# A two-block transformer kernel in float32: h_lo's last two tiles lie 32 bytes further down

## The chip, the cores and the metric

The kernel runs on one core of a Trainium2 chip. The time is that of the device from start to end, in microseconds (us), as the median of three runs. Besides the times there is one profiled execution, from which all rows below are taken.

## The reference, cut to what matters

Two transformer blocks are computed on 256 tokens of width 2048, all in float32. What the change touches is the left factor of most of the large products, h:

```python
def pool_mixer_layer(x, norm_g, w_in, w_group, scale, w_out):
    h = rmsnorm(x, norm_g)
    proj = h @ w_in                      # 2048 x 8192
    ...
def mla_layer(x, k, v, ...):
    h = rmsnorm(x, norm_g)
    proj = h @ w_in                      # 2048 x 2560
    ...
    return x + (o * jax.nn.silu(gate)) @ w_out
def second_block(x, c, ...):
    h = rms_norm(x, norm_attn[l]) * (1.0 + sc1) + sh1
    qa, ka, va, qb, ckv, qi, ki, wi = jnp.split(h @ w_in[l], SPLIT_POINTS, axis=-1)
    ...
    h = rms_norm(x, norm_ffn[l]) * (1.0 + sc2) + sh2
    x = x + g2 * conv_ffn(h, w_up[l], conv_w[l], conv_b[l], w_down[l])   # 2048 x 11264, 5632 x 2048
    return rms_norm(x, norm_final)
```

## The kernel before, in words

A float32 product is made of three products of a narrower type, float32r. Each factor is split into a high part and a low part; hi x hi, lo x hi and hi x lo are summed. The weights stream in from memory in slabs of 2 x 512 columns (or 4 x 256). SyncE's queue loads a slab into `raw`, ScalarE writes its high part `w_hi` (line 660), VectorE the low part `w_lo` (line 1228), each in a ring of four. The activations are kept transposed, as 16 tiles of 128 features by 256 tokens, in `h_hi` and `h_lo`. They are filled anew for each layer, two tiles at a time, by ScalarE (`h_hi`) and VectorE (`h_lo`, lines 1295, 1298 and 1649), which is the only way in which VectorE is concerned with the change.

`gemm` makes one product of four output tiles. It goes over eight slabs, and slab s uses the tiles 2s and 2s + 1 of h. Within a slab there are 16 matmuls with `w_hi`, which alternate between `h_hi` and `h_lo`, and then 8 with `w_lo`, which read `h_hi` alone. The weights are the stationary factor, and the tile of h (256 columns, 1024 bytes in each partition) is the moving one. All are issued by the helper on line 1953. Slabs of 4 x 256 columns use four tiles of h and give two output tiles, so the third and the fourth tile alternate with the first and second. Products whose moving factor is something else (`pool`, `y`, `y_mid`, `f`, `hk`, `c`, `q`, `mixw`) are made in the same manner; `hk_hi` and `hk_lo` are a copy of h for the key and value product and lie in two other homes.

The order on each engine is written out by hand, with semaphores. It runs through the first layer (from the start to about 630 us in the profile), key and value product and attention layer (to about 1010 us), the second block's attention (to about 1330 us) and its FFN, the feed-forward part (to the end). The small matmuls of the attention stages are put between the slabs.

The memory is laid out by hand as well: `home(start, end)` gives addresses in order, each tensor at a multiple of 32 bytes. From H_AT = 147776 on there are `h_hi` and `h_lo`. Both are `Parted`: the first 14 tiles, a gap of 8 floats (32 bytes), the last two tiles under the name `..._tail`, and a gap behind. So `h_hi` takes 16640 bytes and `h_lo` begins at H_AT + 16640. `Parted` picks the tensor by the index of the tile; no access goes over the boundary. In what follows the slab of tiles 14 and 15 is called the tail slab.

Of the kernel before, what the change touches and what calls it, by code (L numbers as in the profile page):

```python
# [16 lines left out]
F32R = mybir.dt.float32r  # L17
# [5 lines left out]
P = 128  # L23
TOK = 256
HALVES = TOK // P
D = 2048
KD = D // P
# [177 lines left out]
def two_block_kernel(nc, t, out, cols):  # L205

    fixed = ExitStack()
    with fixed:
        def home(start, end):

            at = [start]

            def sb(name, shape, dt=F32):
                tile = nc.alloc_sbuf_tensor_at(name, shape, dt, offset=at[0])
                at[0] += -(-4 * int(np.prod(shape[1:])) // 32) * 32
                assert at[0] <= end, (name, at[0], end)
                return tile

            return sb
# [34 lines left out]
        h_sb = home(H_AT, FAR)  # L254
        def h_parts(name, gap):

            main = h_sb(name, [P, H_TAIL, TOK], F32R)
            h_sb(name + "_gap", [P, 8])
            tail = h_sb(name + "_tail", [P, KD - H_TAIL, TOK], F32R)
            h_sb(name + "_end", [P, gap])  # L260
            return Parted(main, tail, H_TAIL)

        h_hi = h_parts("h_hi", 56)
        h_lo = h_parts("h_lo", 8)
        mod_sb = home(MOD_RAW_AT, SB_END)
        mod_raw = [mod_sb(f"mod_raw{s}", [P, 1024]) for s in range(MOD_RING)]

# [2323 lines left out]
```

How the kernel before makes its waits and increments, by code:

```python
            def load_mod():  # L455
                top = LATE_MODS if slabs.total() < LATE_MODS_AT else 6 * MOD_TILES
                while mod_loads.total() < MOD_RING or mod_loads.total() < min(top, MOD_RING + mod_due(slabs.total() - RING - 1)):
                    n = mod_loads.total()
                    if n == LATE_MODS:
                        sp.wait_ge(att[1]["mix_lo"], TILES)
                        load_row()
                    v, j, slot = n // MOD_TILES, n % MOD_TILES, n % MOD_RING
                    if n >= MOD_RING:
                        sp.wait_ge(mod_used, n + 1 - MOD_RING)
                    sp.dma_start(mod_raw[slot][:, :], t["w_mod_2"][bass.ds(v * D + (j // 2) * P, P), bass.ds((j % 2) * 1024, 1024)])\
                        .then_inc(mod_landed[slot], 16)
                    mod_loads.step()
# [1 line left out]
            def load(src, k, n):  # L470
                sp.wait_ge(lo_ready, slabs.value(1))
                s = slabs.slot(RING)
                sp.dma_start(raw[s][:, 0:k * n].rearrange("p (k n) -> p k n", k=k),
                             src.rearrange("(k p) n -> p k n", p=P)).then_inc(raw_landed[s], 16)
                after_load()
# [1 line left out]
            def load_heads(src):  # L478
                sp.wait_ge(lo_ready, slabs.value(1))
                s = slabs.slot(RING)
                sp.dma_start(raw[s][:, :].rearrange("p (h d) -> p h d", d=HD), src.rearrange("h p d -> p h d")).then_inc(raw_landed[s], 16)
                after_load()
```

## Time and profile before

| | us |
|---|---|
| median of three runs | 2078.72 |
| lowest and highest | 2076.68, 2080.64 |
| profiled execution | 2075.5 |
| its span, first to last instruction | 2073.7 |
| TensorE busy in it | 2049.6 |
| VectorE busy | 1566.9 |
| ScalarE busy | 1030.2 |

The profile is a page with tables, and views of the trace behind it. In the page and the views PE is TensorE's matmuls, PEld its loads of weights, DVE VectorE, ACT ScalarE. A row of a group reads: line, engine, operation, output and inputs, shapes, count, then busy time and the mean duration of one in ns, then the idle time before them and what ended it. Matmuls overlap, so that the duration of one is longer than the distance to the next. In a row of the timeline the first number is the start in us, the second the time to the end, and the last the number of equal instructions merged in it.

### The profile page before, as it was taken

The page shows a single profiled execution, that of the slowest core. Times are in us where ns is not written, and L with a number is a line of the kernel's source. Part 1 is how long each engine was busy: PE and PEld are TensorE (multiplying, and loading weights), DVE is VectorE, ACT ScalarE, POOL GpSimd, SP SyncE. Part 2 cuts the span into 40 slices and gives each one's busy share as a digit, 9 for nine tenths or more (in the row PEclk, how much of TensorE's full clock was granted, in tenths as well). Part 3 has the DMA queues.
Part 4 walks back from the last instruction along what each step waited for, and adds up shares of the span by engine and source line. Part 5 has one row for each costly group of instructions (what it writes and reads, how often), then busy time and mean ns, then how long its engine had stood idle before and what let it go on. Part 6 is the DMA issues. An engine that isn't in the chain of part 4 may idle for free.

```text
span 2073.7 us, 41240 instructions
## 1 busy us (share of the span) xinstructions
PE 2049.6 (99%) x17698; PEld 2019.0 (97%) x17698; DVE 1566.9 (76%) x2256; ACT 1030.2 (50%) x1339; POOL 15.4 (1%) x23
## 2 busy tenths in 40 slices
PE   8999999999999999999999999999999999999998
PEld 7999999999999999999999899999999999999998
DVE  7988788688688888877756686778866666666666
ACT  6444444444445476664567557454444444444444
POOL 1000000000000000000000000000000000000000
PEclk9999999999999999999999999999999999999999
DMA  8898888889686788748654754568866666666663
GB/s 272 293 354 278 292 306 304 260 288 324 225 296 204 236 302 297 232 163 280 202 158 120 191 170 135 191 225 321 317 215 192 195 193 193 193 193 193 194 193 122
DMA packets 248749, 483.01 MB, mean 233 GB/s; under 512 B 26347, under 2 KB 59735, under 8 KB 248311
## 3 DMA queue, kind: packets, MB, share of 16 engines
q1 hardware_dynamic: 247807, 480.16, 71.3%
q8 instruction: 139, 2.28, 0.4%
q14 instruction: 43, 0.35, 0.1%
q0 software_dynamic: 528, 0.15, 0.0%
q10 hardware_dynamic: 232, 0.06, 0.0%
HBM read 478.17 MB, written 8.44 MB: 235 GB/s over the span
## 4 chain that ended last, share of the span: by engine, by line
PE 93%; DVE 4%; ACT 1%; DMA 1%; issue 0%; DVEq 0%; SPq 0%; ACTq 0%
PE acc L1953 87%; PE side L1953 3%; PE sums L1953 2%; DVE w_lo L1228 2%; PE sums L2228 1%; DVE tmp L1283 0%; DVE mod_raw L1216 0%; ACT w_hi L660 0%; DMA raw<-in_a_w_in 0%; DVE h_lo L1295 0%; DVE tmp L1285 0%; DVE xT L1358 0%; PE sums L2036 0%; DVE h_lo L1298 0%; PE acc L2088 0%
## 5 line engine op out<-in xcount | busy, mean ns | idle before, releaser
L1228 DVE TENSOR_TENSOR w_lo<-raw,w_hi 128x1024 fp32r<-128x1024 f32 x681 | 830.6, 1229 | 412.8 <-ACT w_hi L660 406.0
L660 ACT ACTIVATE w_hi<-raw 128x1024 fp32r<-128x1024 f32 x681 | 718.3, 1059 | 817.9 <-PE acc L1953 704.4
L1953 PE MATMUL acc<-h_hi,w_hi 128*128 128x256 f32 x3166 | 749.5, 280 | 6.8 <-ACT h_hi L744 2.4
L1953 PE MATMUL acc<-h_lo,w_hi 128*128 128x256 f32 x3166 | 741.1, 277 | 0.0
L1953 PEld LDWEIGHTS acc<-h_hi,w_hi 128*128 128x128 f32 x3166 | 594.7, 189 | 17.4 <-issue 12.7
L1953 PEld LDWEIGHTS acc<-h_lo,w_hi 128*128 128x128 f32 x3166 | 593.4, 188 | 0.1
L1953 PE MATMUL acc<-h_hi,w_lo 128*128 128x256 f32 x3166 | 430.0, 278 | 0.2 <-DVE w_lo L1228 0.2
L1953 PEld LDWEIGHTS acc<-h_hi,w_lo 128*128 128x128 f32 x3166 | 392.9, 188 | 0.4 <-DVE w_lo L1228 0.4
L1216 DVE SCALAR_TENSOR_TENSOR mod_raw<-mod_raw,silu_row 128x1024 f32<-128x1024 f32 x192 | 234.1, 1219 | 5.4 <-DMA mod_raw<-in_w_mod 5.3
L1953 PE MATMUL acc<-f_hi,w_hi 128*128 128x256 f32 x704 | 164.6, 277 | 0.0
L1953 PE MATMUL acc<-f_lo,w_hi 128*128 128x256 f32 x704 | 164.3, 276 | 0.0
L1953 PEld LDWEIGHTS acc<-f_hi,w_hi 128*128 128x128 f32 x704 | 132.2, 188 | 0.1
L1953 PEld LDWEIGHTS acc<-f_lo,w_hi 128*128 128x128 f32 x704 | 132.2, 188 | 0.0
L1953 PE MATMUL acc<-h_hi_tail,w_hi 128*128 128x256 f32 x434 | 105.6, 281 | 0.0
L1953 PE MATMUL acc<-h_lo_tail,w_hi 128*128 128x256 f32 x434 | 105.5, 281 | 0.0
L1953 PE MATMUL acc<-f_hi,w_lo 128*128 128x256 f32 x704 | 94.2, 276 | 0.0
L1953 PE MATMUL acc<-y_hi,w_hi 128*128 128x256 f32 x384 | 89.5, 276 | 0.0
L1953 PE MATMUL acc<-y_lo,w_hi 128*128 128x256 f32 x384 | 89.5, 276 | 0.0
L1953 PEld LDWEIGHTS acc<-f_hi,w_lo 128*128 128x128 f32 x704 | 86.4, 188 | 0.0
L1953 PEld LDWEIGHTS acc<-h_hi_tail,w_hi 128*128 128x128 f32 x434 | 81.6, 188 | 0.5 <-issue 0.5
L1953 PEld LDWEIGHTS acc<-h_lo_tail,w_hi 128*128 128x128 f32 x434 | 81.5, 188 | 0.0
L1953 PEld LDWEIGHTS acc<-y_hi,w_hi 128*128 128x128 f32 x384 | 72.1, 188 | 0.0
(350 smaller groups left out, 2485.1 us busy)
## 6 DMA issues: line engine op xcount, KB each, us to landing
mod_raw<-in_w_mod SPq DMA_DIRECT2D x192, 512.0 KB, 6.4
raw<-in_w_up SPq DMA_DIRECT2D x176, 512.0 KB, 4.4
raw<-in_a_w_in SPq DMA_DIRECT2D x128, 512.0 KB, 5.1
raw<-in_w_down SPq DMA_DIRECT2D x88, 512.0 KB, 4.5
raw<-in_a_w_out SPq DMA_DIRECT2D x64, 512.0 KB, 5.6
raw<-in_w_in SPq DMA_DIRECT2D x52, 512.0 KB, 3.8
raw<-in_b_w_in SPq DMA_DIRECT2D x40, 512.0 KB, 5.1
raw<-in_a_w_group SPq DMA_DIRECT2D x32, 512.0 KB, 5.2
```

The source lines that it names most:

```text
L660: last = act.activation(w_hi[s][:, :], raw[s][:, :], ACT.Copy)
L1216: dve.scalar_tensor_tensor(x[:, :], x[:, :], 1.0, silu_row[:, half * 1024:(half + 1) * 1024], ALU.mult, ALU.mult, accum_out=mod_part[:, v ...
L1228: last = dve.tensor_tensor(w_lo[s][:, :], raw[s][:, :], f32(w_hi[s][:, :]), ALU.subtract)
L1953: return pe.matmul(o, lhsT, rhs, start=start, stop=stop, skip_group_check=True)
L2228: last = pe.transpose(o[:, e, c], pr[:, e, c], ident)
```

## The change

`h_lo` becomes one tensor of 16 tiles. It begins at the same address as before; its tiles 0 to 13 stay where they were, and its tiles 14 and 15 lie 32 bytes further down, right behind tile 13. `h_hi` keeps its gap. Nothing lies behind `h_lo` that would move: the next home has a fixed address. No instruction is added or removed, and no order is changed.

```diff
         h_hi = h_parts("h_hi", 56)
-        h_lo = h_parts("h_lo", 8)
+        h_lo = h_sb("h_lo", [P, KD, TOK], F32R)
         mod_sb = home(MOD_RAW_AT, SB_END)
```

## Rows read from the trace of the kernel before

**Rows 1.** The page: span, busy time and shares of engines, chain that ended last.

```profile
span 2073.7 us, 41240 instructions
...
PE 2049.6 (99%) x17698; PEld 2019.0 (97%) x17698; DVE 1566.9 (76%) x2256; ACT 1030.2 (50%) x1339; POOL 15.4 (1%) x23
...
PE 93%; DVE 4%; ACT 1%; DMA 1%; issue 0%; DVEq 0%; SPq 0%; ACTq 0%
```

**Rows 2.** Costliest groups of the page: count, busy us, mean ns, idle before.

```profile
L1953 PE MATMUL acc<-h_hi,w_hi 128*128 128x256 f32 x3166 | 749.5, 280 | 6.8 <-ACT h_hi L744 2.4
```

**Rows 3.** Windows: stretch, its us, PE busy (x matmuls), clock, DMA share, GB/s.

```profile
28.00:630.00 602.00, 601.78 (x5274) 1.00 0.85 290
...
655.00:1330.00 675.00, 670.36 (x5667) 1.00 0.67 210
...
1359.00:2054.00 695.00, 695.00 (x6106) 1.00 0.68 212
```

**Rows 4.** Groups of PE within 655 to 1330 us.

```profile
L1953 PE MATMUL acc<-h_hi,w_hi 128*128 128x256 f32 x1024 | 249.8, 286 | 3.3 <-DVE kq L1530 1.5 <-ACT h_hi L744 1.2 <-DVE xT L1358 0.7
```

**Rows 5.** Tile h_lo_tail: count, duration ns min/median/max, first and last start.

```profile
L1953 PE MATMUL acc<-h_lo_tail,w_hi x434: 277/281/285, 35.9 to 2014.3; 128*128 128x256 f32 x144, 128*80 128x256 f32 x1
L1298 DVE SCALAR_TENSOR_TENSOR h_lo_tail<-tmp,mod,h_hi_tail x4: 479/486/488, 1024.1 to 1347.3; 128x256 fp32r<-128x256 f32 x4
```

**Rows 6.** Timeline of PE (start us, us) in the FFN, round a tail slab.

```profile
1486.88 1.07 PE L1953 MATMUL acc<-h_hi,w_lo 128*128 128x256 f32 x8
1487.79 0.28 PE L1953 MATMUL acc<-h_hi_tail,w_hi 128*128 128x256 f32 x1
...
1489.68 1.11 PE L1953 MATMUL acc<-h_hi_tail,w_lo 128*128 128x256 f32 x8
1490.62 0.28 PE L1953 MATMUL acc<-f_hi,w_hi 128*128 128x256 f32 x1
...
1491.22 0.28 PE L1953 MATMUL acc<-f_lo,w_hi 128*128 128x256 f32 x1
...
1498.82 0.28 PE L1953 MATMUL acc<-f_hi,w_hi 128*128 128x256 f32 x1
...
1501.54 0.28 PE L1953 MATMUL acc<-f_hi,w_hi 128*128 128x256 f32 x1
```

**Rows 7.** The same, where the FFN begins.

```profile
1355.55 1.10 PE L1953 MATMUL acc<-h_hi,w_lo 128*128 128x256 f32 x8
1356.49 0.28 PE L1953 MATMUL acc<-h_hi_tail,w_hi 128*128 128x256 f32 x1
...
1359.33 0.29 PE L1953 MATMUL acc<-h_hi,w_hi 128*128 128x256 f32 x1
...
1361.18 1.07 PE L1953 MATMUL acc<-h_hi,w_lo 128*128 128x256 f32 x8
```

**Rows 8.** The same, a slab of four rows of tiles (12 to 15).

```profile
1213.36 0.28 PE L1953 MATMUL acc<-h_hi,w_hi 128*128 128x256 f32 x1
...
1213.81 0.28 PE L1953 MATMUL acc<-h_hi_tail,w_hi 128*128 128x256 f32 x1
...
1214.28 0.28 PE L1953 MATMUL acc<-h_hi,w_hi 128*128 128x256 f32 x1
...
1214.75 0.28 PE L1953 MATMUL acc<-h_hi_tail,w_hi 128*128 128x256 f32 x1
...
1215.22 0.40 PE L1953 MATMUL acc<-h_hi,w_lo 128*128 128x256 f32 x2
```

**Rows 9.** The same, first slab of the key and value product.

```profile
630.57 0.28 PE L1953 MATMUL acc<-hk_hi,w_hi 128*128 128x256 f32 x1
...
632.43 1.07 PE L1953 MATMUL acc<-hk_hi,w_lo 128*128 128x256 f32 x8
```

**Rows 10.** The same, products over y: five slabs in a row.

```profile
185.85 1.07 PE L1953 MATMUL acc<-y_hi,w_lo 128*128 128x256 f32 x8
...
196.73 1.07 PE L1953 MATMUL acc<-y_hi,w_lo 128*128 128x256 f32 x8
```

## The prediction

> **What bounds the kernel now.** I read the page first, for who is busy: of a span of 2073.7 us TensorE works 2049.6 us, and 93% of the chain that ended last is its own [rows 1]. VectorE, the next, has 24% to spare. The largest matmul group has 6.8 us of idle time before it for 749.5 us of work [rows 2]. Then the windows: from 28 to 630 us and from 1359 to 2054 us TensorE is busy all the time at the full granted clock, which is the level of 2.4 GHz, while the DMA share is 0.85 and 0.68 [rows 3]. So in these 1297 us nothing ends last but TensorE's own stream, and the time is the number of matmuls times the distance between two starts. 695.00 us over 6106 matmuls is 113.8 ns each [rows 3]. The durations of some 280 ns are of no use for this, since matmuls overlap; what counts is the distance of starts, the **pace**, and it is read from the timeline.
>
> **The pace** has more than one value. A slab (24 matmuls of 256 columns: 16 with w_hi, 8 with w_lo) of f tiles runs from 1498.82 to 1501.54, 2.72 us, 113.3 ns a matmul. The slab of tiles 14 and 15, the tail slab, runs from 1487.79 to 1490.62, 2.83 us or 117.9 ns, and its 16 matmuls with w_hi, from 1487.79 to 1489.68, take 118.1 ns each [rows 6]. Is it the place of the tiles in memory, or that this is the last slab of a product, when the other engines turn to the sums? The products over y answer: four slabs each, so one in four is a last one, and four slabs in a row take 196.73 - 185.85 = 10.88 us, 2.72 each, the last one included [rows 10]. The place remains. H_AT is 64 x 2309, and h_lo starts at H_AT + 16640 = 64 x 2569; main tiles lie at multiples of 64 bytes, tail tiles 32 bytes past one.
>
> Two more things can be seen. After a tail slab the first five matmuls, which read f tiles at multiples of 64, take 1490.62 to 1491.22, 120 ns each, and then the pace is 113.3 again [rows 6]. And the slow pace also occurs where nothing is shifted: the eight matmuls of tiles 12 and 13 with w_lo before 1356.49 need 0.94 us, 117.5 ns, and eight after the tail slab need 1.07 us from first start to last end instead of 1.10 [rows 7]. So TensorE has a fast and a slow pace for the same tiles, it stays in the one that it is in, and the tail slab, itself slow, was followed by the fast one. The FFN (the feed-forward part) then keeps it for 695 us.
>
> **The change part by part.** It removes the 32-byte gap between h_lo's tiles 13 and 14. h_lo's main tiles, h_hi with its tail and all else stay where they are: h_lo starts at the same address before and after. No instruction, wait, queue or size is added or taken away. What moves is the operand of 434 matmuls with w_hi [rows 5] and the target of seven VectorE instructions that fill the tail tiles, such as the four of 486 ns [rows 5].
> - Those seven: I take their cost as nothing, since their inputs and sizes are the same. If each were 5% longer or shorter, at about half a microsecond each, and all of it on the path, that is 7 x 0.025 = 0.2 us either way.
> - The 434 matmuls. 49 slabs have 8 of them, nine slabs of four tiles each have 4, one narrower slab has 6: 392 + 36 + 6 = 434. In each such stretch a matmul of h_hi's tail, still shifted, alternates with one of h_lo's, no longer shifted; the 8 with w_lo read h_hi's tail alone and are as before. No row shows this very mixture. **Lower bound:** every h_lo matmul falls to the fast pace and its neighbours don't change: 434 x (118.1 - 113.3) ns = 2.1 us less. **Upper bound:** a matmul at a multiple of 64 after a shifted one costs what the five after a tail slab do, 120 ns, and so does its partner: 868 x 1.9 ns = 1.6 us more [rows 6].
> - Between these, two nearer rows. The slab of tiles 12 to 15 changes between places every four matmuls: its first four, unshifted, take 0.45 us (112 ns each), the four shifted 0.47, the next four unshifted ones 0.47 as well, not 0.45, and the next shifted four 0.47 [rows 8]. Once disturbed, unshifted tiles run at 117.5 ns among shifted ones, so a mixture gains next to nothing. The key and value product alternates, matmul by matmul, between two homes, hk_hi at FAR and hk_lo at MID, and its 16 with w_hi take 632.43 - 630.57 = 1.86 us, 116.3 ns each, 1.8 below the tail's [rows 9]; by this row the change saves 868 x 1.8 ns = 1.6 us. The first row is nearer, having the same tiles and the same 32 bytes; the second is nearer in its rhythm. I take 0.5 us less, and keep -2.1 to +1.6.
> - The slab after the tail: the last 8 matmuls before it, all on h_hi's shifted tail, are unchanged, so I leave its 16 with w_hi at 1.85 us [rows 7], 0.04 above the fast pace. If this goes away, 50 times 0.04 is 2 us less; the reverse is the rival below.
>
> The Trainium skill speaks against any effect. SBUF — State Buffer, under Specifications (TRN2), gives SBUF lines of 16 bytes and a penalty for each move to another line. By that rule a tile of 1024 bytes covers 64 lines with the shift and without it, so the change would do nothing. The 118.1 against 113.3 ns of rows 6 don't agree with it.
>
> **Sum.** The profiled execution took 2075.5 us, its span of 2073.7 and 1.8 around it. Minus 0.5 it is 2075.0. The median of the three runs is 2078.72, 3.2 above the profiled one; minus 0.5 it is 2078.2. The runs themselves differ by 4 us (2076.68 to 2080.64), so this gain would not be seen: about 0.2%, 4.2 us, is what a measurement of this kernel can tell from no change.
>
> **The rivals.**
> 1. Place plays no part, and the tail slab is slow for another reason, or the lines of 16 bytes are all that counts. Then the time is as before, 2078.7. Rows 10 speak against it; it moves neither sign.
> 2. The slow side: **the tail slab no longer hands over the fast pace.** The shifted stretch is what precedes the change to the fast pace in rows 7. Now its first 16 matmuls are mixed, and the 8 shifted ones left may be too few to bring it about. The place is the slab after each tail slab; it decides as soon as that slab keeps 117.5 to 118 ns instead of returning within five matmuls. In the FFN 21 tail slabs after 1359 hold 504 of 6106 matmuls; the other 5602 at 4.4 ns more make 24.6 us. From 28 to 630 us 5274 matmuls less 16 tail slabs (384) and the 384 on y_mid leave 4506, or 19.8 us [rows 3]. Both: 2078.7 + 44.4 = 2123; one alone: about 2100. Against it: rows 6 and 7 show the handover from a fast and from a slow state alike, and rows 8 show shifted and unshifted tiles mixed without the slab growing slower than a tail slab. For it: nothing in the trace has this mixture followed by eight shifted ones.
> 3. The fast side: from 655 to 1330 us TensorE often falls into the slow pace after small matmuls of the attention stages. There 1024 matmuls of h_hi with w_hi [rows 4] have as many of h_lo and of w_lo beside them, 3072, up to 4.4 ns too slow each, 13.5 us. A different tail could draw these anew. If half of it goes, with the 2.1 us above, the time is about 2070; the same redraw can lose, since not all of the stretch is slow.
>
> **How the numbers follow.** Forecast (mixture between the bounds, handover kept) 0.72; rival 1 0.08; rival 2 0.12, of which half is the whole 44 us; rival 3 0.07; 0.01 is left for losses of another kind. The likeliest is the forecast: 2078.2 us. Its own range is the bounds, -2.1 to +1.6, with 2 us for the runs on either side: 2074.6 to 2082.3. To hold 8 in 10 a little of the redraw in the middle is taken in: 2074.0 to 2084.0; the whole of rival 2 stays outside. Within 0.2% (2074.6 to 2082.9) lie the forecast and rival 1 nearly whole, 0.79; faster are rival 3 and a sliver, 0.08; slower 0.13.
>
> **What would show it.** In the changed trace a tail slab's 16 matmuls with w_hi take 1.86 to 1.91 us. 1.85 or less says that the two places are paid for separately (lower bound). The slab after it: its eight with w_lo take 1.07 us if the handover holds, 1.10 if rival 2 is right, and the window of the FFN is then about 720 us instead of 695. Rival 3 shows between 655 and 1330 us only. If tail slabs keep 118.1 ns to the tenth while h_lo lies at a multiple of 64, the pace is set by h_hi alone or by something other than place. The prediction is wrong as soon as the FFN's pace leaves 113.8 ns.

## The result and the profile after

| | before | after |
|---|---|---|
| median, four runs each on one chip (us) | 2078.85 | 2096.9 |
| lowest and highest | 2076.68, 2080.64 | 2091.66, 2101.38 |
| profiled execution, its span | 2075.5, 2073.7 | 2101.38, 2099.5 |

The ratio is 1.0092 (95% interval 1.008 to 1.0104): 18 us slower. The forecast was 2078.2 us, within 2074 to 2084. It was wrong. The profiled execution of the changed kernel is the slowest of its four, while that of the kernel before is faster than any of its four, so the two traces differ by 25.8 us where the medians differ by 18. What follows explains the 25.8; why executions of one kernel differ by up to 10 us was not traced.

The page of the changed kernel: the span, the busy times, the chain that ended last, and three groups (busy us, mean ns of one, idle before).

```profile
span 2099.5 us, 41240 instructions
...
PE 2075.2 (99%) x17698; PEld 2045.2 (97%) x17698; DVE 1569.9 (75%) x2256; ACT 1030.8 (49%) x1339; POOL 15.4 (1%) x23
...
PE 92%; DVE 5%; ACT 1%; DMA 1%; issue 1%; POOL 0%; DVEq 0%; ACTq 0%; POOLq 0%
...
L1953 PE MATMUL acc<-h_hi,w_hi 128*128 128x256 f32 x3166 | 758.8, 282 | 6.4 <-ACT h_hi L744 2.4
L1953 PE MATMUL acc<-f_hi,w_hi 128*128 128x256 f32 x704 | 169.9, 281 | 0.0
L1953 PE MATMUL acc<-y_hi,w_hi 128*128 128x256 f32 x384 | 89.5, 276 | 0.0
```

The instructions are the same, and the idle time before h's matmuls is 6.4 us against 6.8 [rows 2]. VectorE is busy 3.0 us longer, with 25% of the span to spare. TensorE's busy time grew by 25.6 us, the span by 25.8 [rows 1]. The second group says more; in the kernel before it reads:

```profile
L1953 PE MATMUL acc<-f_hi,w_hi 128*128 128x256 f32 x704 | 164.6, 277 | 0.0
```

The f tiles were not moved by a byte, and their matmuls became longer, from a mean of 277 ns to 281. The y tiles, which are not moved either, stayed at 276. So it is not the moved tile alone that pays.

The windows of the changed kernel (stretch, its us, PE busy and matmuls, clock, DMA share, GB/s), to be laid beside [rows 3]:

```profile
28.00:630.00 602.00, 602.00 (x5226) 602.00 (x5225) 490.44 (x614) 264.70 (x256) 2.41 (x1) 1.00 0.84 288
655.00:1330.00 675.00, 670.30 (x5641) 642.52 (x5641) 505.95 (x865) 405.33 (x702) 0.00 (x0) 0.99 0.66 209
1359.00:2054.00 695.00, 695.00 (x5967) 695.00 (x5966) 477.51 (x609) 292.15 (x278) 0.00 (x0) 1.00 0.68 212
```

The granted clock is full here as before, at 2.4 GHz (0.99 to 1.00), and the DMA share is the same to 0.01. In equal time fewer matmuls start: 48 fewer in the first layer (5.5 us at 115 ns), 26 fewer in the middle (3 us), 139 fewer in the FFN (16 us at 116.5 ns). That is 24.5 of the 25.8 us.

Where they are lost, the timeline of TensorE shows (start us, us to the end, count). First a tail slab of the FFN that is entered at the fast pace, and the slabs behind it; then the next tail slab:

```profile
1387.06 1.07 PE L1953 MATMUL acc<-h_hi,w_lo 128*128 128x256 f32 x8
1387.96 0.28 PE L1953 MATMUL acc<-h_hi_tail,w_hi 128*128 128x256 f32 x1
1388.08 0.28 PE L1953 MATMUL acc<-h_lo,w_hi 128*128 128x256 f32 x1
...
1389.86 1.11 PE L1953 MATMUL acc<-h_hi_tail,w_lo 128*128 128x256 f32 x8
...
1392.70 1.10 PE L1953 MATMUL acc<-h_hi,w_lo 128*128 128x256 f32 x8
...
1409.66 1.10 PE L1953 MATMUL acc<-h_hi,w_lo 128*128 128x256 f32 x8
1410.60 0.28 PE L1953 MATMUL acc<-h_hi_tail,w_hi 128*128 128x256 f32 x1
...
1412.49 1.11 PE L1953 MATMUL acc<-h_hi_tail,w_lo 128*128 128x256 f32 x8
1413.44 0.28 PE L1953 MATMUL acc<-h_hi,w_hi 128*128 128x256 f32 x1
...
1415.28 1.07 PE L1953 MATMUL acc<-h_hi,w_lo 128*128 128x256 f32 x8
```

Look at the eight with w_lo: 1.07 us ahead of the first tail slab, 1.10 in the seven slabs behind it, 1.07 again behind the second. A tail slab that is entered fast is left slow, and one that is entered slow is left fast. It has become a switch: of the 38 tail slabs of the two stretches 19 are entered fast and left slow, and 19 are entered slow and left fast, in turn. In the kernel before, 36 of 37 were left fast; behind the other one, at 36 us, the next slab has a late start of 491 ns. In the FFN 150 of the 227 slabs that are not tail slabs are slow now (none of 233 before), in the first layer 56 of 186 (none of 187; both without the slabs on y_mid). At 24 x 4.4 ns each that is 15.8 and 5.9 us. More than half of the FFN's are slow since the switch stands so: seven slabs of h lie between a block's two tail slabs and are fast, fifteen (eight of f, seven of h) lie from there to the next block's first and are slow.

### The profile page after: what moved, and what is told of

Read it like the earlier page. It is cut to its first block, busy times and chain, and to the rows that moved or that the text cites. A ratio compares the mean times of both kernels' runs of the same rounds, so it can differ in the third digit from the quotient of the medians.

```text
span 2099.5 us, 41240 instructions
## 1 busy us (share of the span) xinstructions
PE 2075.2 (99%) x17698; PEld 2045.2 (97%) x17698; DVE 1569.9 (75%) x2256; ACT 1030.8 (49%) x1339; POOL 15.4 (1%) x23
## 4 chain that ended last, share of the span: by engine, by line
PE 92%; DVE 5%; ACT 1%; DMA 1%; issue 1%; POOL 0%; DVEq 0%; ACTq 0%; POOLq 0%
PE acc L1953 86%; PE side L1953 3%; DVE w_lo L1228 2%; PE sums L1953 2%; DVE mod_raw L1216 1%; PE sums L2228 1%; ACT w_hi L660 0%; DVE tmp L1285 0%; DMA raw<-in_kv_w_b 0%; DVE tmp L1283 0%; DVE xT L1358 0%; DMA vec_rows<-in_b_q_norm_g 0%; PE sums L2036 0%; DVE h_lo L1298 0%; DVE h_lo L1295 0%
## 5 line engine op out<-in xcount | busy, mean ns | idle before, releaser
L1228 DVE TENSOR_TENSOR w_lo<-raw,w_hi 128x1024 fp32r<-128x1024 f32 x681 | 831.2, 1229 | 434.7 <-ACT w_hi L660 427.1
L1953 PE MATMUL acc<-h_lo,w_hi 128*128 128x256 f32 x3600 | 855.7, 279 | 0.0
L1953 PE MATMUL acc<-h_hi,w_hi 128*128 128x256 f32 x3166 | 758.8, 282 | 6.4 <-ACT h_hi L744 2.4
L1953 PEld LDWEIGHTS acc<-h_lo,w_hi 128*128 128x128 f32 x3600 | 677.7, 189 | 0.1
L1953 PE MATMUL acc<-h_hi,w_lo 128*128 128x256 f32 x3166 | 435.8, 280 | 0.0
L1953 PEld LDWEIGHTS acc<-h_hi,w_lo 128*128 128x128 f32 x3166 | 398.6, 189 | 0.0
L1953 PE MATMUL acc<-f_hi,w_hi 128*128 128x256 f32 x704 | 169.9, 281 | 0.0
L1953 PE MATMUL acc<-f_lo,w_hi 128*128 128x256 f32 x704 | 169.9, 281 | 0.0
L1953 PEld LDWEIGHTS acc<-y_lo,w_hi 128*128 128x128 f32 x384 | 72.1, 188 | 0.0
L1362 DVE SCALAR_TENSOR_TENSOR xT<-acc,mod,xT 128x256 f32<-128x256 f32 x168 | 69.5, 476 | 1.3 <-PE acc L1953 1.3
```

What stands on the lines that cost most here:

```text
L1228: last = dve.tensor_tensor(w_lo[s][:, :], raw[s][:, :], f32(w_hi[s][:, :]), ALU.subtract)
L1362: last = dve.scalar_tensor_tensor(x, acc[s][:, n, :], mod[:, scale, bass.ds(m + n, 1)], x, ALU.mult, ALU.add)
L1953: return pe.matmul(o, lhsT, rhs, start=start, stop=stop, skip_group_check=True)
```

## The experiments

The times below are medians of the runs that are named, or single runs where it says so; a ratio is taken against the kernel before on the same chip, whose medians were 2077.3 to 2078.45 us.

Two readings were open. **A:** each tail slab works on the pace that follows it, and what it leaves depends on the order of shifted and unshifted operands in it; with no shifted tile there would be no reset at all. **B:** a shifted tile anywhere is bad for its neighbours, or the time depends on the place of h_lo as such, so that taking the last shift away too would bring the time back.

**e1: no tile shifted.** h_hi is one piece as well; a gap of 256 bytes behind it keeps h_lo where it is.

```diff
-        h_hi = h_parts("h_hi", 56)
+        h_hi = h_sb("h_hi", [P, KD, TOK], F32R)
+        h_sb("h_hi_end", [P, 64])
```

> Neither h_hi nor h_lo has a gap; h_lo begins at the same address as before and after. Theory A (shifted tiles are slow themselves, but they are also the only thing that moves TensorE from the slow pace of 117.8 ns a matmul to the fast one of 113.3 and back): the first layer starts fast and stays fast, tail slabs included, so 28 to 630 us of the kernel before get 16 x 0.145 = 2.3 us shorter; the FFN is entered at the slow pace, as before, and nothing takes it out of it: 6106 matmuls at 117.8 instead of 113.8 ns, 24 us more. Sum against before: about +22 us, 2100 us. Theory B (what costs is only a mixture of two places in one slab; an unshifted tile has no memory of it): every slab at 113.3 ns, some 7 us less than before, 2072 us.

Measured: 2098.14 us, ratio 1.0133 (1.0077 to 1.019), four runs from 2092.1 to 2120.72. The windows and the timeline are those of its fastest run; the timeline lies between the last two windows:

```profile
28.00:630.00 602.00, 602.00 (x5297) 601.93 (x5297) 497.27 (x623) 269.57 (x262) 4.80 (x2) 1.00 0.84 291
...
1359.00:1498.00 139.00, 139.00 (x1229) 139.00 (x1229) 114.98 (x150) 66.51 (x63) 0.00 (x0) 1.00 0.84 294
1500.00:2054.00 554.00, 554.00 (x4706) 554.00 (x4705) 359.99 (x461) 222.84 (x213) 0.00 (x0) 1.00 0.59 189
```

```profile
1497.99 1.07 PE L1954 MATMUL acc<-f_hi,w_lo 128*128 128x256 f32 x8
1498.91 0.39 PE L1954 MATMUL acc<-f_hi,w_hi 128*128 128x256 f32 x1
1499.14 0.28 PE L1954 MATMUL acc<-f_lo,w_hi 128*128 128x256 f32 x1
...
1500.90 1.10 PE L1954 MATMUL acc<-f_hi,w_lo 128*128 128x256 f32 x8
```

Reading B falls. Without any shift the first layer is the fastest of all kernels (5297 matmuls), and so is the FFN's start: 139 us over 1229, 113.1 ns. Then one distance is 230 ns instead of 113, from 1498.91 to 1499.14, and from there to the end the pace is 554 us over 4706, 117.7 ns, on the same addresses. Nothing brings it back. (That the FFN began fast was not what A had expected; no run shows why.) So an unshifted stream keeps the pace that it has, a small disturbance can change it, and the 32 bytes act as a reset.

Such a disturbance changes the pace only sometimes. In e2, which comes next, the distance behind the very same matmul is 220 ns, and the fast pace stays:

```profile
1505.03 0.39 PE L1954 MATMUL acc<-f_hi,w_hi 128*128 128x256 f32 x1
1505.25 0.28 PE L1954 MATMUL acc<-f_lo,w_hi 128*128 128x256 f32 x1
...
1506.96 1.07 PE L1954 MATMUL acc<-f_hi,w_lo 128*128 128x256 f32 x8
```

The kernel before has a distance of 223 ns two slabs further on, at 1507.01 us, and stays fast; e8 has two, of 234 and 221 ns, at that same place, is slow from there, and is fast again behind the next tail slab, at 1535 us. That is what the reset is worth. Late starts at other moments would explain why e1's four runs lie up to 29 us apart, but only one of them was profiled.

**e2: the changed layout, the tail slab in another order.** The eight h_lo tiles first, then all 16 shifted ones without a break. LEAD is the number of shifted matmuls ahead of h_lo's, 0 here.

```diff
+                    if x_hi is h_hi and s * k + x0 >= H_TAIL:
+                        pairs_of = [(i, c0, rows, kk) for i, (c0, rows) in enumerate(tiles) for kk in range(k)]
+                        order = [(x_hi, q) for q in pairs_of[:LEAD]] + [(x_lo, q) for q in pairs_of] + [(x_hi, q) for q in pairs_of[LEAD:]]
+                        for x_part, (i, c0, rows, kk) in order:
+                            mm(a[0:rows, i, :], hi[:, kk, c0:c0 + rows], x_part[:, s * k + kk + x0, :])
 ...
```

> The layout of the kernel after, but in the tail slab the 8 matmuls of h_lo with w_hi (unshifted) come first, then the 8 of h_hi with w_hi and the 8 of h_hi with w_lo (shifted) in one run of 16. Theory A1 (the pattern of starts in a run of shifted matmuls repeats every eight, and the place in it where the run ends decides the pace that follows): a run that starts from unshifted matmuls and ends after 16 ends at the same place as the 24 of the kernel before, so every product after a tail slab is fast, and 8 matmuls a slab are no longer shifted: 2078.8 less about 49 x 8 x 4.5 ns = 1.8, some 2077 us. Theory A2 (h_lo's tail has to be shifted as well, or 24 shifted ones are needed): the paces alternate as in the kernel after, 2097 us.

Measured: 2076.12 us over ten runs, ratio 0.9994 (0.9985 to 1.0004). The whole loss is gone with the changed layout still in place. Timeline of e2, a tail slab:

```profile
1993.76 1.07 PE L1954 MATMUL acc<-h_lo,w_hi 128*128 128x256 f32 x8
1994.67 1.10 PE L1954 MATMUL acc<-h_hi_tail,w_hi 128*128 128x256 f32 x8
1995.61 1.11 PE L1954 MATMUL acc<-h_hi_tail,w_lo 128*128 128x256 f32 x8
1996.55 0.28 PE L1954 MATMUL acc<-h_hi,w_hi 128*128 128x256 f32 x1
...
1998.40 0.84 PE L1954 MATMUL acc<-h_hi,w_lo 128*128 128x256 f32 x6
```

The eight of h_lo take 0.91 us (fast), the shifted ones 0.94 per eight, and the slab behind takes 1.85 us for its 16 with w_hi, as in [rows 7]. So the place of h_lo's tail is no loss by itself: with it unchanged, the order in the tail slab takes the loss away.

**e5, e6, e11: how many shifted ones in a row.** The same kernel with LEAD 3, 8 and 4: the last unbroken run of shifted matmuls is 13, 8 and 12 long, all else is equal. In the tail slabs of the kernel before, the distances of starts repeat every eight matmuls (116, 122, 117, 117, 122, 116, 116, 120 ns and near it), three times in the 24; the question was whether the place in this pattern at which the run stops decides.

```diff
-LEAD = 0
+LEAD = 3
```

> As e2_grouped (the layout of the kernel after), but three matmuls of h_hi with w_hi come ahead of the 8 of h_lo: the tail slab has the same 24 matmuls and the same 16 shifted ones, of which 3 stand at its start and 13 in one run at its end. Theory A1 (the place in the pattern of eight starts at which the run of shifted matmuls ends decides the pace that follows): 13 = 8 + 5 ends at the same place as the tail slab of the kernel after when it is entered fast (last start distances 116, 122), so that the slow pace follows a tail slab at least in every other product: 2095 to 2122 us. Theory A2 (what counts is that shifted matmuls are grouped, or that their run is long enough to clear out the mixture): 2076 us, as e2_grouped.

> As e2_grouped, but the order in the tail slab is 8 of h_hi with w_hi (shifted), 8 of h_lo with w_hi (unshifted), 8 of h_hi with w_lo (shifted). Theory A1: a run of 8 ends where a run of 16 ends (last distances 116, 120), so the fast pace follows: 2076 us. If a run has to be longer than that of the kernel after to be sure (A2), this one, with 8 at its end as there, behaves like the kernel after: 2097 us.

> As e5_run13 with four matmuls of h_hi ahead of h_lo's eight instead of three: the run at the end is 12 = 8 + 4. The pattern read in the kernel before is 116, 118, 117, 117, 122, 116, 116, 120 ns; place 5 (13, 5) ends after the long distance of 122 and was slow, place 8 after 120 was fast, place 7 fast as well (the first tail slab of the FFN before). Place 4 was not seen. Since the long distance after it is missing I expect the unshifted matmuls to take it and to be slow: 2095 to 2124 us; fast, 2076 us, would put the border between places 4 and 5.

e5, e6 and e11 are single runs:

| | last shifted run | us | matmuls in 28 to 630 | in 1359 to 2054 |
|---|---|---|---|---|
| before | 24 | 2078.7 | 5274 | 6106 |
| e2 | 16 | 2076.12 | 5246 | 6111 |
| e6 | 8 | 2076.11 | 5275 | 6108 |
| e5 | 13 | 2123.85 | 5114 | 5882 |
| e11 | 12 | 2117.41 | 5128 | 5902 |

Windows and timeline of e5:

```profile
28.00:630.00 602.00, 602.00 (x5114) 602.00 (x5113) 478.54 (x598) 256.92 (x249) 0.00 (x0) 1.00 0.82 281
...
1359.00:2054.00 695.00, 694.34 (x5882) 694.17 (x5882) 478.01 (x624) 291.20 (x285) 0.00 (x0) 1.00 0.66 207
```

```profile
2036.84 0.52 PE L1954 MATMUL acc<-h_hi_tail,w_hi 128*128 128x256 f32 x3
2037.19 1.10 PE L1954 MATMUL acc<-h_lo,w_hi 128*128 128x256 f32 x8
2038.14 0.76 PE L1954 MATMUL acc<-h_hi_tail,w_hi 128*128 128x256 f32 x5
2038.73 1.11 PE L1954 MATMUL acc<-h_hi_tail,w_lo 128*128 128x256 f32 x8
2039.68 0.29 PE L1954 MATMUL acc<-h_hi,w_hi 128*128 128x256 f32 x1
```

Three matmuls moved within each tail slab cost some 47 us against e2. It is not the number of shifted ones (16 in all of them), nor that more of them are better (8 are enough, 13 are not). In this table lengths that are multiples of eight lead to the fast pace, and 12 and 13 don't. The length alone is not the rule, though: the changed kernel ends every tail slab with a run of eight as well, behind a mixture, and leaves half of them slow. What the kernels do share is where the pattern stands at the end. The last distances of a tail slab, and what it leaves (medians of the FFN, in ns, from the starts in the traces):

| | last four distances | left |
|---|---|---|
| before, e2, e6 | 122, 116, 116, 120 | fast |
| after, entered slow | 122, 116, 116, 120 | fast |
| after, entered fast | 123, 117, 117, 122 | slow |
| e5 | 123, 117, 117, 122 | slow |

The tail slabs of both long stretches, in these kernels and in e7 to e10 below, bear it out: where the third and second distance from the end add up to 231 or 232 ns, 238 of 241 are left fast, and the three others have a late start of 491 to 683 ns in the slab behind; where they add up to 234 or 235 ns, 95 of 95 are left slow. Two that are entered slow, in e2 and e8, show neither and are left fast. e11 ends at other places, with 239 or 240, and is left slow. When nearly all slabs of the two stretches are slow the time is that which rival 2 had priced: 2123. Rival 2's "too few" was wrong: eight would have been enough, had they begun at the right place.

**e10: a run of five.** The changed layout; the tail slab goes eight h_hi with w_hi, three h_hi with w_lo, eight h_lo, five h_hi with w_lo.

```diff
+                            if tail_slab and len(pairs_of) - i * k - kk == LAST:
+                                for j, c, r, q in pairs_of:
+                                    mm(a[0:r, j, :], hi[:, q, c:c + r], x_lo[:, s * k + q + x0, :])
 ...
```

> The layout and the 24 matmuls of e6_run8, but the 8 unshifted ones of h_lo come three matmuls later, after 3 of those with w_lo: the tail slab ends with a run of 5 shifted ones. Theory A1 (the pattern has a period of eight): 5 ends where 13 ended, and the slow pace follows every tail slab or nearly every one: 2095 to 2124 us. Against it (long runs of 8 and more reset, whatever their length, and 13 was slow because of the 3 at its start): no forecast but that 5 is no more like 13 than like 8; about 2076 or 2097 us.

Measured: 2121.17 us, one run. Windows of e10:

```profile
28.00:630.00 602.00, 602.00 (x5114) 602.00 (x5113) 479.79 (x601) 257.09 (x248) 0.00 (x0) 1.00 0.83 282
...
1359.00:2054.00 695.00, 694.84 (x5892) 694.66 (x5891) 476.30 (x619) 290.55 (x282) 0.00 (x0) 1.00 0.66 208
```

Slow in both stretches from the first tail slab on, as at 13: five and 13 are the same place in a pattern of eight, and e10's tail slabs end with 117, 117, 122 ns too. The rival for e5, that its three shifted ones at the start made it slow, doesn't fit this, since e10's run of five has 11 shifted ones ahead of the unshifted eight.

**e4, e7: the mirror image.** Now h_hi is one piece and h_lo has the shifted tail, so that only eight matmuls of a tail slab are shifted. In e4 they alternate with h_hi's as the kernel has them; in e7 the eight are moved to the end of the slab, behind those with w_lo.

```diff
-        h_hi = h_parts("h_hi", 56)
-        h_lo = h_sb("h_lo", [P, KD, TOK], F32R)
+        h_hi = h_sb("h_hi", [P, KD, TOK], F32R)
+        h_sb("h_hi_end", [P, 64])
+        h_lo = h_parts("h_lo", 8)
```

> h_hi one piece, h_lo with the 32-byte gap: the shifted tail is read by 8 matmuls of 24, each between two unshifted ones, and the 8 with w_lo are unshifted. Theory A1: the run of shifted matmuls at the end of the slab has length zero; the eight unshifted ones settle in one of the two paces before the slab ends. If a mixture ends at one place for each pace on entry, it is a fixed rule again; I expect the slow pace to be kept or reached oftener than in the kernel after, 2090 to 2105 us. Theory B (number of shifted matmuls alone): 434 instead of 868 + 434, so a third of the tail's cost of 6 us, and 2073 us.

> The layout of e4_mirror (h_hi one piece, h_lo with the 32-byte gap; 2122 us in the usual order), with the tail slab's order changed: 8 of h_hi with w_hi, 8 of h_hi with w_lo, and last the 8 of h_lo with w_hi, the only shifted ones, in one run. Theory A1: a run of 8 that starts from unshifted matmuls and ends the slab leaves the fast pace behind, whatever pace it is entered with; only 8 of 24 are shifted, and 16 x 4.5 ns a slab are saved against the kernel before: 49 x 16 x 4.5 = 3.5 us, some 2075 us. If the layout of h_hi is what matters: 2100 us or more.

Measured: e4 2122.14 us (one run), slower than the 2090 to 2105 expected. In the first layer nothing was fast from the second tail slab on, and in the FFN nothing after the few slabs that come ahead of its first tail slab: 5110 and 5888 matmuls in the two windows. The single shifted ones between unshifted ones are no reset: all 38 tail slabs there are left slow. e7: 2075.33 us over ten runs, ratio 0.999 (0.998 to 0.9999), with 6119 matmuls in the FFN's window. Its timeline, a tail slab:

```profile
1991.23 1.07 PE L1954 MATMUL acc<-h_hi,w_hi 128*128 128x256 f32 x8
1992.14 1.07 PE L1954 MATMUL acc<-h_hi,w_lo 128*128 128x256 f32 x8
1993.05 1.10 PE L1954 MATMUL acc<-h_lo_tail,w_hi 128*128 128x256 f32 x8
1993.99 0.28 PE L1954 MATMUL acc<-h_hi,w_hi 128*128 128x256 f32 x1
```

Sixteen at 113.3 ns (0.907 us per eight) and eight at 117.5: the same reset with a third of the shifted matmuls. Again the same tiles at the same addresses, and the order alone makes 47 us. The length of the run and its place at the end of the slab were changed together here.

**e3, e12: how far the tail is shifted.** The changed layout with the gap ahead of h_hi's tail at 64 and at 256 bytes instead of 32.

```diff
-            h_sb(name + "_gap", [P, 8])
+            h_sb(name + "_gap", [P, 16])
```

(64 for 16 in e12. The gap behind h_hi's tail shrinks by as much, so that h_lo stays where it is.)

> The kernel after with a gap of 64 bytes in h_hi instead of 32 (h_lo one piece at the same address). If the place counts modulo 64 bytes, this is the layout without any shift: tail slabs at the pace of their neighbours, first layer fast throughout, FFN slow throughout at 117.8 ns, about 2100 us. If any gap between tiles 13 and 14 or the distance from h_hi's to h_lo's tail counts, tail slabs stay at some 118 ns and the paces alternate: 2097 us, with fast stretches in the FFN.

> As e3_gap64 with a gap of 256 bytes in h_hi: its tail tiles lie at 64 modulo 256 again, like h, y, pool and f, while in e3 they lay at 128 modulo 256. If the place modulo 256 decides (as the y_mid experiment says), the tail is no different from its neighbours: tail slabs at 113.3 ns in a fast stretch and 117.8 in a slow one, no handover to the fast pace at any tail slab, and the state of the FFN is left to chance as in e1_both_flat: 2072 to 2122 us. If any gap, or any distance between the tails of h_hi and h_lo other than before, makes the tail slow and a reset: tail slabs at 117 to 118 ns, the slab after at 114 to 115, 2075 us, as e3.

Measured: e3 2074.68 us, e12 2089.51, one run each. e3 was expected to be like e1, with no slower tiles, on the guess that what counts is the address modulo 64. It was not so. Timeline of e3:

```profile
1989.89 0.28 PE L1953 MATMUL acc<-h_hi_tail,w_hi 128*128 128x256 f32 x1
...
1991.76 1.11 PE L1953 MATMUL acc<-h_hi_tail,w_lo 128*128 128x256 f32 x8
1992.71 0.29 PE L1953 MATMUL acc<-h_hi,w_hi 128*128 128x256 f32 x1
...
1994.54 1.07 PE L1953 MATMUL acc<-h_hi,w_lo 128*128 128x256 f32 x8
```

Shifted by 64 bytes the tail is nearly as slow as by 32 (1.87 us for its 16 with w_hi, 1.11 for the w_lo; 117.5 against 118.1 ns a matmul), and it leads to the fast pace with the alternating order too (all 37 tail slabs of the two stretches, 6108 matmuls in the FFN). Its tail slabs end with 119, 121, 117, 117 ns, so the distances of the table above are those of the 32-byte shift alone. At 256 bytes, in e12, tail slabs run at their neighbours' pace and reset nothing:

```profile
28.00:630.00 602.00, 602.00 (x5118) 602.00 (x5117) 480.06 (x601) 257.01 (x248) 0.00 (x0) 1.00 0.83 282
...
1359.00:2054.00 695.00, 694.49 (x6125) 694.30 (x6124) 490.82 (x636) 302.38 (x292) 0.00 (x0) 1.00 0.68 216
```

One stretch is slow, one fast, and in both the pace changes at no tail slab. In the first layer it turns slow at a late start of 153 ns, at 40.99 us; in the FFN one of 213 ns, at 1517.75, turns it slow, and one of 164 ns, at 1523.49, fast again: the largest FFN count of all kernels stands beside one of the smallest first layers. h's main tiles start at 64 modulo 256 (H_AT is 147776, a tile is 1024 bytes). Starts at 96 and 128 modulo 256 cost 117.5 to 118 ns, those at 64, and at 64 once more after 256 bytes, can run at 113.3. The Trainium skill's line of 16 bytes (SBUF — State Buffer, Specifications (TRN2)) does not tell these apart, since all of these starts are multiples of 32; here the measurements decide.

**e8, e9: the address alone, and both together.** The 16 slabs on y_mid are slow in the kernel before, from 541 to 587 us; the eight with w_lo of one of them:

```profile
543.70 1.10 PE L1953 MATMUL acc<-y_mid_hi,w_lo 128*128 128x256 f32 x8
```

y_mid starts at 192 modulo 256. e8 is before with 128 bytes put ahead of it; e9 is e7 with the same.

```diff
+        mid("y_mid_gap", [P, 32])
```

> The kernel before with a gap of 128 bytes ahead of y_mid_hi and y_mid_lo, whose 384 matmuls run at 117.8 ns though they lie at multiples of 64 bytes; they lie at 192 modulo 256 and then at 64, as h, y, pool and f do. If the place modulo 256 sets the pace: these 16 slabs at 113.3 ns, 1.7 us less in the stretch from 541 to 587 us. If a slow pace entered by chance is carried through (no tail slab is between): they stay at 117.8 ns.

> e7_mirror_last together with the 128-byte gap of e8_ymid128. Both theories that held add up: against the kernel before, 49 tail slabs with 16 matmuls at 113.3 instead of 118.1 ns (3.5 us by the sum, 2.1 in the first comparison of e7) and y_mid's 384 matmuls at 113.3 instead of 117.8 ns (1.7 us): 2078.8 - 4 to 5 = 2074 us, ratio about 0.998. If the two interfere (a fast y_mid changes what the layer after it meets), the gain is that of e7 alone, ratio 0.999.

Measured: e8 2076.66 us (one run). Its timeline, two slabs of y_mid in a row:

```profile
543.79 1.07 PE L1954 MATMUL acc<-y_mid_hi,w_lo 128*128 128x256 f32 x8
...
546.51 1.07 PE L1954 MATMUL acc<-y_mid_hi,w_lo 128*128 128x256 f32 x8
```

2.72 us a slab instead of 2.83, on tiles that have nothing to do with h. It is not the luck of one run: the 16 slabs take 117.8 ns a matmul in all 12 kernels without the 128 bytes, whatever pace came before, and 113.3 in the two with them. e8's time by itself cannot be told from that of the kernel before. e9: 2073.61 us over eleven runs, ratio 0.9981 (0.9972 to 0.999), the lowest median of all versions, 0.2% below the kernel before.

## Why the prediction was wrong

**What bounds the kernel: right.** The time is the number of matmuls times the distance of starts, on the way up as well; 24.5 of 25.8 us are read from the same windows, at the same clock and DMA share to 0.01.

**Two paces, and that place makes them: right, but for the measure.** I read the place as a multiple of 64 bytes or 32 past one. e3's tail lies at a multiple of 64 and takes 117.5 ns, and y_mid, at 192 modulo 256, does so at 117.8; what fits all runs is the start modulo 256. e8, e3 and e12 show the place without h_lo, and e1's two windows show 113.1 and 117.7 ns for tiles that all lie alike. Rival 1 is out.

**The VectorE term: right.** VectorE's idle time and its waits play no part in the difference; no group of TensorE has over 0.4 us more idle time before it.

**The mixture: within its bounds, with the wrong sign.** A tail slab's 16 matmuls with w_hi take 1.90 us (1387.96 to 1389.86) or 1.89 (1410.60 to 1412.49), against 1.89 in [rows 6]. A whole tail slab went from 118.1 to 118.4 ns a matmul; over all of them that is 0.3 us more, where I had 0.5 less within -2.1 and +1.6. Both numbers are small beside the result.

**The step that failed is the last of the parts: "the last 8 matmuls before it ... are unchanged, so I leave its 16 with w_hi at 1.85 us".** It took the handover to hang on the matmuls next to it. What the runs show is that it hangs on the place at which a longer sequence stops: e5, e10 and e11 have at least five shifted ones next to the handover, e5 eight of the same kind in the same order as e2, and all three are left slow. In the changed kernel itself, the same eight leave 19 tail slabs fast and 19 slow. Rows 6 and 7, on which I leaned, were both of the same case, 24 shifted ones, a multiple of eight; two entries with the same sequence say nothing about another sequence. Rows 8, which I held against rival 2, show how long a mixture takes, and not what it leaves behind.

**Rival 2** had the mechanism, the place and the sign to look for, and got 0.12. Its price per matmul, 4.4 ns, was right, and its whole, 2123 us, is near what e4, e5 and e10 measured (2122.14, 2123.85, 2121.17). Its reason was off as well: it is not that eight shifted ones are too few. The change itself gave 18 us in the medians (26 in the profiled pair) and not 44, since only every second tail slab hands over slow. That a switch is a third possibility beside "kept" and "lost" was not among the cases. The FFN's window counts 139 matmuls fewer; as 16 us it is 711 for 695, where the full rival had 720.

**Rival 3** named the stretch where a small part of the loss fell: the middle lost some 26 matmuls, 3 us.

**The range** left out rival 2 on purpose. The mistake was its chance: no row spoke on the sequence, and in hindsight a price of 25 to 44 us that hung on a row which nobody had seen deserved more than an eighth.

## What to carry to other kernels

When a kernel's matmuls follow each other without a gap, read the distance of their starts slab by slab, and not their durations. If the same tiles show two distances, look for what sets the pace afresh before moving anything, and count what an edit does to the sequence ahead of that point, not only the instructions next to it. A loss of this kind is repaired in order as well as in layout: with e4's layout, moving the eight shifted matmuls to the end of the tail slab was worth 47 us.

## What the runs showed of the hardware

- Matmuls of 256 columns of float32r, each with its own load of weights, start every 113.3 or every 117.5 to 118 ns at the same full granted clock. Which of the two depends on the moving tile's start modulo 256 bytes (64 can be fast; 96, 128 and 192 were not) and, at 64, on what ran before. The starts modulo 256 are the four that were measured, no more, and the weights' ring never moved.
- The pace is kept: for 555 us in e1. A single late start (a distance of 153 to 234 ns) can change it, to slow (e1, e8, e12) or to fast (e12), and need not (before, e2).
- A run of tiles shifted by 32 bytes has distances that repeat every eight matmuls. With 122, 116, 116, 120 ns at the end of the slab the fast pace follows, with 117, 117, 122 the slow one. Runs of 16 and 24 gave the first, 5 and 13 the second; runs of 8 gave the first behind unshifted tiles (e6, e7), and either behind a mixture (the changed kernel). That the place in the pattern causes what follows is the plainest reading of this; no run sets it apart from the order that makes it.
- Which part of the chip has this state, and why it has a period of eight, no run here shows. A run in which the weights' addresses are moved and the tiles' kept was not made.
